# Two weight splits moved ahead of an expert turn, filler products on TensorE, and the memory gain on the load queue

## The reference

```python
mem_n = rms_norm(mem, g_mem)              # g_mem is "the memory norm's vector"
...
kv = (mem_n @ w_kv).reshape(b, n_mem, 2, M_HEADS, M_HEAD_DIM)
...
logits = jnp.matmul(ht, w_router)         # 256 tokens, 8 experts
top_v, top_i = lax.top_k(logits, TOP_K)   # the best two
top_w = jax.nn.softmax(top_v, axis=-1)
...
y = (jax.nn.silu(xb @ w_gate[e]) * (xb @ w_up[e])) @ w_down[e]   # one expert, up to 128 tokens at a time
```

## Time and profile before

| | us |
|---|---|
| time, median of 3 runs | 1816.9 (1815.12 to 1817.38) |
| time of the profiled execution | 1816.69 |
| its span (first to last instruction) | 1814.9 |
| opening, to the first product with weights | 0 to 14.07 |
| norm of layer 1 to the first product of the turns | 757.8 to 786.6 |
| eight turns | 786.6 to 1801.7 |
| last scatter and norm | 1801.7 to 1814.9 |

### The profile page before, as it was taken

One profiled execution on the slowest core, in us unless ns is written; L12 is line 12 of the kernel. 1 busy time (PEld: TensorE's weight loads), 2 busy tenths in 40 slices (PEclk: granted clock), 3 DMA queues, 4 the chain that ended last, 5 costly groups with the idle time before them and its releaser, 6 DMA issues.

```text
span 1814.9 us, 28902 instructions
## 1 busy us (share of the span) xinstructions
PE 1762.9 (97%) x9812; PEld 1513.9 (83%) x9812; DVE 1390.5 (77%) x1484; ACT 1192.3 (66%) x1421; POOL 23.8 (1%) x49
## 2 busy tenths in 40 slices
PE   7999999999999999889999999999999999999997
PEld 6888899999988889778888888888888888888886
DVE  6675475455466755679999899899899899898997
ACT  5465544444445656367777777777777777877775
POOL 2000000000000000000000000000000000000000
PEclk9999999999999999979999999999999999999999
DMA  8543366666665334859989999999899899899990
GB/s 323 160 116 115 121 230 187 185 187 187 185 184 160 113 111 133 299 210 370 369 313 370 336 340 368 337 344 367 315 370 362 315 368 365 310 370 339 341 360 23
DMA packets 213867, 479.20 MB, mean 264 GB/s; under 512 B 14768, under 2 KB 16832, under 8 KB 213296
## 3 DMA queue, kind: packets, MB, share of 16 engines
q1 hardware_dynamic: 212592, 474.80, 75.3%
q0 software_dynamic: 1216, 3.61, 0.6%
HBM read 475.20 MB, written 3.15 MB: 264 GB/s over the span
## 4 chain that ended last, share of the span: by engine, by line
PE 92%; ACT 4%; DVE 2%; issue 2%; DMA 0%; POOL 0%; POOLq 0%; ACTq 0%; DVEq 0%
PE ps L1657 83%; PE ps L2027 2%; PE ps L2060 1%; PE ps L1884 1%; ACT probs L1006 1%; PE ps L1867 1%; PE ps L2041 1%; PE ps L1854 1%; PE ps L1709 0%; DVE wlo L1181 0%; ACT whi L871 0%; PE ps L1856 0%; ACT probs L998 0%; ACT gates L1039 0%; DVE row_max L1383 0%
## 5 line engine op out<-in xcount | busy, mean ns | idle before, releaser
L1181 DVE TENSOR_TENSOR wlo<-raw,whi 128x1024 fp32r<-128x1024 f32 x766 | 915.5, 1220 | 297.9 <-ACT whi L871 287.3
L871 ACT ACTIVATE whi<-raw 128x1024 fp32r<-128x1024 f32 x766 | 795.3, 1055 | 317.2 <-PE ps L1657 307.0
L1657 PE MATMUL ps<-whi,xg_hi 128*128 128x512 f32 x896 | 358.4, 400 | 4.3 <-DVE wlo L1181 4.3
L1657 PE MATMUL ps<-wlo,xg_hi 128*128 128x512 f32 x896 | 354.2, 395 | 0.0
L1657 PE MATMUL ps<-whi,xg_lo 128*128 128x512 f32 x896 | 354.2, 395 | 0.0
L1657 PE MATMUL ps<-hT_hi,whi 128*128 128x256 f32 x896 | 259.5, 290 | 4.3 <-ACT gates L881 2.9
L1657 PE MATMUL ps<-hT_lo,whi 128*128 128x256 f32 x896 | 254.1, 284 | 0.0
L1657 PE MATMUL ps<-hT_hi,wlo 128*128 128x256 f32 x896 | 253.9, 283 | 0.0
L1657 PEld LDWEIGHTS ps<-whi,xg_hi 128*128 128x128 f32 x896 | 169.0, 189 | 42.4 <-DVE wlo L1181 4.5
L1657 PEld LDWEIGHTS ps<-wlo,xg_hi 128*128 128x128 f32 x896 | 168.9, 189 | 40.0
L1657 PEld LDWEIGHTS ps<-whi,xg_lo 128*128 128x128 f32 x896 | 169.1, 189 | 38.0
(11 more groups left out here) (311 smaller groups left out, 2197.6 us busy)
## 6 DMA issues: line engine op xcount, KB each, us to landing
raw<-in_w_down_exp SPq DMA_DIRECT2D x200, 512.0 KB, 5.1
raw<-in_w_gate_exp SPq DMA_DIRECT2D x184, 512.0 KB, 5.0
raw<-in_w_up_exp SPq DMA_DIRECT2D x160, 512.0 KB, 5.3
raw<-in_w_in SPq DMA_DIRECT2D x72, 512.0 KB, 3.7
kM<-in_w_up_exp SPq DMA_DIRECT2D x40, 512.0 KB, 5.6
raw<-in_w_gate_dense SPq DMA_DIRECT2D x28, 512.0 KB, 4.3
raw<-in_w_up_dense SPq DMA_DIRECT2D x28, 512.0 KB, 4.4
raw<-in_w_down_dense SPq DMA_DIRECT2D x28, 512.0 KB, 4.3
```

The costliest lines, as they stand in the source:

```text
L871: s.activation(whi[n % SPLIT][:, 0:w], raw[tile(key)][:, 0:w], ACT.Copy).then_inc(chunk_hi, 1)
L1181: v.tensor_tensor(wlo[n % SPLIT][:, 0:w], raw[tile(key)][:, 0:w], whi[n % SPLIT][:, 0:w].bitcast(F32), ALU.subtract).then_inc(chunk_split, 1)
L1657: ins = mm(o, lhsT, rhs, start=start and i == 0, stop=stop and i == 2, skip_group_check=True)
```

## The change

There are three edits, and tensors that change places.

1. **Two splits ahead.** `turn_starts` holds the splits of chunks 0 and 1 of a turn on ACT and on DVE (`AHEAD` = 2). It stands once before the loop, ahead of `gathered_hi(0)` and `gathered_lo(0)`, and once at the end of the loop's body, for the next turn; the body then starts with chunk 2. Since the last turn splits two chunks for a turn that doesn't come, SP loads two more chunks (the first expert's) at the end.
2. **Filler products.** `keep_busy(n)` multiplies the identity by itself n times, in float32, into columns 512 to 639 of `ps1`, where nothing is read. PE does 13 ahead of the first transposes, 2 after the router, 12 ahead of the ranks, 8 ahead of the gather and 4 behind it. They wait for nothing but `constants`, and stand ahead of the waits of the step that follows.
3. **The memory gain.** SP issues the load of `g_mem` behind the two tiles of `mem` and ahead of the first chunks, with a semaphore of its own; POOL no longer issues it and starts with `ident`.

```diff
+AHEAD = 2
...
             for t in range(NT):
                 sp.dma_start(normed[:, t, :], A["mem"][0, P * t:P * (t + 1)]).then_inc(mem_loaded[t], 16)
+            sp.dma_start(gain[:, :], A["g_mem"].partition_broadcast(P)).then_inc(mem_gain_loaded, 16)
...
+            for key in moe_loop[0:AHEAD]:
+                load(key, turns, weights_of=0)
...
-            load_gain(0, A["g_mem"])
...
+            def turn_starts(turn):
+                for key in moe_loop[0:AHEAD]:
+                    hi_of(key, turn)
+
+            turn_starts(0)
             gathered_hi(0)
             with s.Fori(0, turns) as e:
-                done_m = [0]
+                done_m = [AHEAD]
...
                 gathered_hi(e + 1)
+                turn_starts(e + 1)
...
+            def keep_busy(n):
+                for _ in range(n):
+                    mm(ps[1][:, 512:512 + P], ident[:, :], ident[:, :], start=True, stop=True)
+
             pe.wait_ge(constants, 3)
+            keep_busy(13)
             transposes(("memT",), 0)
...
             ins.then_inc(psum_full[2], 1)
+            keep_busy(2)
             wait_free(pe, ("router_T",))
...
             ins.then_inc(psum_full[2], 1)
+            keep_busy(12)
             pe.wait_ge(masks_ready, 1)
...
+            keep_busy(8)
             pe.wait_ge(normed_split, 1)
             pe.wait_ge(routed_sem, 1)
             gather()
+            keep_busy(4)
             pe.wait_ge(turns_ready, 1)
```

More of the change, by code:

```diff
@@ L499, in trunk_kernel @@
         assert len(raw) == DEEP
+        xg_hi = sb("xg_hi", [P, KD, SLOTS], F32R)
+        xg_lo = sb("xg_lo", [P, KD, SLOTS], F32R)
+        actm_hi = [sb(f"actm_hi{i}", [P, 4, SLOTS], F32R) for i in range(2)]
+        actm_lo = [sb(f"actm_lo{i}", [P, 4, SLOTS], F32R) for i in range(2)]
+        y_out_lo = sb("y_out_lo", [P, D], F32R)
+        back = sb("back", [P, TOK], F32R)
+        onehot_next = sb("onehot_next", [P, NT, SLOTS], F32R)
+        silu_m = sb("silu_m", [P, FF_GROUP])
+        act_m = sb("act_m", [P, FF_GROUP])
+        earlier = sb("earlier", [P, P])
+        ones = sb("ones", [P, P])
+        iotaS = sb("iotaS", [P, SLOTS])
         logitsT = sb("logitsT", [EXPERTS, TOK])
@@ L510, in trunk_kernel @@
         route_w = sb("route_w", [P, NT, EXPERTS])
-        earlier = sb("earlier", [P, P])
-        ones = sb("ones", [P, P])
         iota8 = sb("iota8", [P, EXPERTS])
-        iotaS = sb("iotaS", [P, SLOTS])
         route = sb("route", [P, 2 * EXPERTS + 1, 4])
         cur_next = sb("cur_next", [P, 4])
-        y_out_lo = sb("y_out_lo", [P, D], F32R)
         most = sb("most", [P, 1])
@@ L520, in trunk_kernel @@
         turns_i = sb("turns_i", [P, 1], I32)
-        onehot_next = sb("onehot_next", [P, NT, SLOTS], F32R)
-        back = sb("back", [P, TOK], F32R)
         slot_w = sb("slot_w", [P, 1])
[L524 to L529, removed]
         moe.close()
@@ L548, in trunk_kernel @@
         router_loaded = sem("router_loaded")
+        mem_gain_loaded = sem("mem_gain_loaded")
         gain_loaded = sem("gain_loaded")
@@ L788, in load_gain @@
             def load_gain(n, row):
-                if n:
-                    pool.wait_ge(norm_done, 2 * n)
+                pool.wait_ge(norm_done, 2 * n)
                 pool.dma_start(gain[:, :], row.partition_broadcast(P)).then_inc(gain_loaded, 16)
-            load_gain(0, A["g_mem"])
             nc.gpsimd.memset(ident[:, :], 0.0).then_inc(constants, 1)
@@ L1199, in norm_apply @@
                 eng.wait_ge(rstd_ready, NT * n + t + 1)
-                eng.wait_ge(gain_loaded, 16 * (n + 1))
+                if n:
+                    eng.wait_ge(gain_loaded, 16 * n)
+                else:
+                    eng.wait_ge(mem_gain_loaded, 16)
                 v.scalar_tensor_tensor(dst[:, t, :], src[:, t, :], rstd[:, t:t + 1], gain[:, :],
@@ L1597, in add_scattered, with turn_starts @@
                     v.tensor_tensor(x[:, t, :], area(key)[:, :], x[:, t, :], ALU.add).then_inc(x_added, 1)
+            def turn_starts(turn):
+                for key in moe_loop[0:AHEAD]:
+                    lo_of(key, turn)
+            turn_starts(0)
             gathered_lo(0)
             with v.Fori(0, turns) as e:
-                done_m = [0]
+                done_m = [AHEAD]
                 def upto(n):
```

## The result

The changed kernel takes 1790.39 us (median of four runs, 1789.58 to 1791.36) beside 1816.06 for the kernel before: a ratio of 0.9858, with a 95% interval of 0.9841 to 0.9875. That is 25.7 us faster, where the prediction took off 9.2 and had a range that ended at 1803.5. The profiled execution has a span of 1789.3 us (1814.9 before).

A forecast was written before the change was run, and what follows sets the result against it. PE, busy 97% of the span, was taken as the bound, so edits pay only through earlier starts or the upper clock. 1816.69 - 0.3 (opening) - 1.2 (opening clock) - 8.0 (routing) + 0.35 (turns) = 1807.5 us, range 1803.5 to 1811.5.

The forecast's parts named there:

- In the turns PE waits for nothing: Turns: four chunks of six products follow each other in 5.59 us, 0.233 us a product, without PE waiting.
- Routing stage: Router to first turn: the clock stays up, turns start 6.9 us earlier, 1.6 more come back, minus 0.5; together 8.0 us.
- chunk 4 cost PE 0.6 for 0.5: First turn: chunk 4, behind chunk 3 and `y_out_lo` on DVE, comes at 785.7, wanted at 785.3; minus 0.5 us.
- The rival of a lost clock in this stage: Routing stage: the clock is lost all the same, only 1.3 us gained there, 1814.2 us in all; chance 0.09.
- long fillers: Rival: a filler costs 0.43 us at the upper clock instead of 0.22, 1810.2 us in all; chance 0.05.
- From turn to turn: Turns: the table load behind chunk 1 delays chunk 2, `y_out_lo` and chunk 4; 0.05 us for each of 7 turns.
- The term of 0.35 us: Turns: loss from the moved table load and jump over 7 turns, 0.35 us, between 0 and 1.4.
- The rival of a slower kernel: Turns: table load and jump lie open on ACT's path, 1.9 us in 8 turns, 1821.9 us; chance 0.03.
- the two terms: Opening: 0.3 us from the gain's load on SP and 1.2 us from the fillers' clock.
- the 1.2 us for the fillers' clock: Opening: 13 fillers raise the clock for the 22 products from 14.07 us; 1.2 us, between 0 and 2.3.
- the rival with a chance of 0.19: Opening: the clock is lost before 13.8 us, the 1.2 us falls away, 1808.7 us; chance 0.19.
- The 0.3 us for the vector on SP: Opening: the memory gain lands sooner on SP's queue, PE starts at about 13.8 instead of 14.07; 0.3 us, between 0 and 0.6.

The follow-up runs named there:

- old_layout: The changed kernel with the allocation order of the kernel before, so all of the change but the new addresses: 1810.5 us, 0.9975 of the kernel before.
- layout_only: The kernel before with only the routing and turn tensors allocated in the changed kernel's order, no instruction changed: 1795.2 us, 0.9887 of the kernel before.
- wshift: The changed kernel with every tensor ahead of `hT`, the split weights among them, moved up by 128 bytes: 1812.1 us, 0.9975 of the kernel before.
- no_ahead: The changed kernel with `AHEAD` = 0, so no splits ahead and no SP loads behind the last turn; fillers and new addresses stay: 1790.0 us.

## Why the prediction was wrong, point by point

**What it left out: the addresses.** The step that failed isn't in its sum. It took the order of allocation, of which the account of the change says that it moves addresses and no instruction, as costing nothing, and gave it no term, no bound and no rival. It was worth 19.8 us, twice the whole forecast. The sentence "In the turns PE waits for nothing [...] 0.233 us a product" took that duration as the product's own. The kernel before held the sign against it: the same shape at the same clock took 390 ns with `actT` and 395 with `xg_lo` in its groups, and nothing asked why:

```profile
L1657 PE MATMUL ps<-whi,actT_lo 128*128 128x512 f32 x112 | 43.6, 390 | 0.0
```

**Routing stage: right.** Forecast 8.0 with the clock up; measured 7.6. The gather took 3.77 us, the five ranks 1.1 as worked out, and chunk 4 cost PE 0.6 for 0.5. What is missing is the clock of the transposes, which the drop at 760.6 to 764.0 made 0.4 us longer. The rival of a lost clock in this stage didn't come true, nor that of long fillers: 12 of them took 2.94 us, 0.245 each for the 0.22 taken. Of the 7.1 us that fell away between the gather's start and the first scatter, taking back the splits ahead costs 3.6 and taking back the fillers 3.3.

**From turn to turn: right mechanism, wrong size.** The prediction named the table load behind chunk 1, `y_out_lo` and chunk 4 in this order, and took 0.05 us a turn, with 0.2 as a bound. Measured at the old addresses it is 0.15 to 0.2 a turn (1005.2 against 1003.8 us from first to last scatter), at the new ones 0.43 (124.35 against 123.92). The term of 0.35 us was 1.4, and with products that are 5 to 6 ns shorter 3.1. The starts of PE's products show the reason. ACT's copy of chunk 1 waits for the first 12 products behind the gather. From the thirteenth to the first of chunk 4, by way of ACT and DVE, it takes 8.40 us in the changed kernel (902.78 to 911.18) and 8.41 in `old_layout` (904.46 to 912.87). PE's own 36 products in between take 8.16 and 8.37 us. So PE waits 0.24 us in one and 0.04 in the other, and starting again costs it another 0.1 in both. The rival of a slower kernel (an open table load in each turn) was a part of the truth, with a quarter of its price.

**Opening: the two terms aren't borne out, nor excluded.** In the changed kernel's trace nothing is left of the 1.2 us for the fillers' clock, as the rival with a chance of 0.19 had it: the products from 13.76 us ran at the lower clock. Other traces differ in this with the same instructions, and the medians with and without the fillers (1790.4 and 1790.1 us) can't tell 1.2 us. The Trainium skill's rule that transposes don't count as busy for the clock (TensorE: Matmul & The Clock Gate, Part 4), by which the rival was to hold, isn't borne out: in `layout_only` the clock was up at the first product, and PE had done nothing but transposes before. The 0.3 us for the vector on SP agree in size (14.07 to 13.76), but with the vector on POOL it is 13.78. By the Trainium skill's rule on the shared engines (Trainium Kernel Development and Optimization, Key Constraints) that term is 0. These two traces agree, though the spread of the first product's start is larger than the term.

**The sum without the addresses.** 1810.5 us measured, 4.5 below the kernel before in the same session, for a forecast of 9.2. Of the 4.7 us between, 1.1 are the turns', and 1.3 the clock at the transposes and up to the ranks in that execution (router to gather took as long as before; gather to first scatter is 7.0 us shorter, as it should be). The other 2.3, with the 1.5 of the opening's two terms among them, can't be placed: the profiled execution of `old_layout` is 6.4 us shorter than that of the kernel before, 1.2 of it ahead of the last product before the router, where the clock fell at other places.

## What to carry to other kernels

An edit that "only" moves tensors in SBUF needs a line of its own in the sum. Before forecasting, list the residue of every matmul operand modulo 256 bytes and compare the mean of groups of equal shape: a group that is a few ns slower than its like at the same clock, with no idle time, is the sign of it. Where work is brought forward once, ahead of a loop, try the first pass written out against the rotated loop: here the rotated loop gave back in its eight turns (3.1 us) most of what it had won once (3.6), and the written-out pass also took the table loads out of the loop. And a term of 1 us in an opening where the clock falls at different places from execution to execution needs more than one trace of either kernel.

## What the runs showed of the hardware

- A float32 product with 512 streamed columns takes 227 ns from one to the next if its two SBUF operands begin at the same residue modulo 256 bytes, and 232 to 234 ns if they differ by 128. It doesn't matter which of them lies at which residue (128/128 and 0/0 are fast, 128/0 and 0/128 slow), and 256 bytes between them cost nothing. It holds for `actT` and `y_out` as for `xg` and `actm`. With 64 bytes between them, one operand then being off a 128-byte line, it is 232 to 235 ns too. Among the slow kernels the time from first to last scatter still lies between 1003.5 and 1006.7 us, unexplained. On 4,200 such products that is 20 us. Why it is so, these runs don't tell. With 256 columns the sign turns (118.9 against 119.9 ns in `wshift`), which stays a hint.
- A loop's body that has copies and SiLU on ACT holds two table loads of 1.28 us a turn, or none if the first turn stands ahead of the loop; a turn then takes 123.65 us instead of the 123.9 of `no_ahead`.
- Transposes alone can bring the clock to its upper level: the 16 from 9.79 us did in `layout_only`, where 22 products then took 2.74 us. In the kernel before, after the same 16 transposes, they took 4.80.
- The clock falls at different places in executions of the same instructions. At the transposes ahead of the router it was 0.77 over the stretch in the changed kernel; in `no_ahead`, with the same work in it, it held, and the stretch took 6.96 instead of 7.41 us (there it fell later, at 780.24):

```profile
753.86:760.82 6.96, 2.77 (x20) 1.93 (x18) 4.23 (x7) 2.19 (x6) 2.35 (x9) 1.00 1.05 394
```

- The same holds for the drop behind the memory's products, which begins between 40.2 and 43.8 us: it is there in eleven of the seventeen traces. The last chunk of products ahead of the router comes between 753.9 and 758.4 us in the traces of these kernels, whose instructions up to there hardly differ. So a difference of 1 or 2 us between two profiled executions says nothing by itself; only stretches between the same two instructions do.
